# Latents of queries and keys evicted raw, the input norm's factor entered later

## The chip, the cores and the metric

The kernel runs on one core of a Trainium2 chip. The metric is the device time of one execution in microseconds; lower is better. Times in this document are device times of whole runs where they are called so, and otherwise times of the one profiled execution, counted from the start of its span.

## The reference

The whole is a transformer block with a linear recurrence and windowed attention, followed by a second block with latent attention, pooling, cross attention and a mixture of experts, all on 256 tokens of width 1024 in fp32. The change lies at the start of the second block:

```python
hn = rms_norm(h, mix_norm_g[l])            # x * rsqrt(mean(x^2) + EPS) * g
z = hn @ w_in[l]
q_lat, kv_lat, k_rope, u_pool, gate_a, gate_b = jnp.split(z, IN_SPLITS, axis=-1)   # 384, 256, 32, 512, ...
q = (rms_norm(q_lat, q_norm_g[l]) @ w_q_up[l]).reshape(B, S, MLA_HEADS, NOPE_DIM + ROPE_DIM)
q_nope, q_rope = q[..., :NOPE_DIM], q[..., NOPE_DIM:]
q_rope = apply_rope(q_rope, cos[:, :, None, :], sin[:, :, None, :])
kv = (rms_norm(kv_lat, kv_norm_g[l]) @ w_kv_up[l]).reshape(B, S, MLA_HEADS, NOPE_DIM + V_DIM)
k_rope = apply_rope(k_rope, cos, sin)
```

`rms_norm` multiplies each token's row by one factor and each column by a gain. A factor per row commutes with the matrix product, so the kernel multiplies `x * g` by `w_in` and brings in the row's factor after the product.

## The kernel before

Five engines run their own instruction lists, ordered by hand and tied by counting semaphores: SyncE (SP) loads weights, TensorE (PE) multiplies, ScalarE (ACT) and VectorE (DVE) prepare operands and empty the PSUM banks, GpSimd does a few fills. The 256 tokens are two tiles of 128 (`t`).

*Weights.* `plan_units` lists all weight pieces in order. For the stretch at hand they are, in this order, `("lat", 0, 0)`, `("lat", 1, 0)`, `("lat", 0, 1)`, `("lat", 1, 1)`, `("lat", 2, 0)`, `("lat", 2, 1)`, then `w_q_up_2` blocks 0 and 1, `w_kv_up_2` blocks 0 and 1, and eight units `gates2`. In a key the second member is the block of columns and the third the half of the rows: block 0 of `lat` is the 384 columns of the queries' latent, block 1 the 288 of the keys' latent and its rotated part, block 2 the 512 of the pooling branch. A unit lands in one of four raw slots, each split into a high part (`act_hi`, ScalarE, `L936`, into one of three `wh` slots) and a remainder (`dve_lo`, VectorE, `L1459`, into `wl`). `act_unit(key)` and `dve_unit(key)` split the unit that comes **two after** `key`. The split of unit i waits until TensorE has used unit i - 3, and the load of unit i waits for the remainder of unit i - 4.

*Matmuls.* `pe_mm3` issues three matmuls for one product (high by high, high by low, low by high; `L461` to `L463`). `pe_tokens` has tokens as output rows; `pe_features` has features as rows and runs four column groups of four row chunks, 48 matmuls a unit. Its dictionary `at` maps a step (two chunks, six matmuls) to work slipped in ahead of it. Groups alternate between the PSUM banks 4, 5 and 6, 7 (`banks_of`): `("lat", 0)`, `("lat", 2)`, `w_q_up_2` block 1 and `w_kv_up_2` block 1 have 4 and 5; `("lat", 1)`, `w_q_up_2` block 0, `w_kv_up_2` block 0 and `gates2` block 0 have 6 and 7. A group starts when the group two before has been evicted (`freed`).

*Turns.* Activations are transposed by TensorE (`pe_turn`, `L524`) into banks, then split by ScalarE (`act_turn`, `L952`, `turn_hi`) and VectorE (`dve_turn`, `L1514`, `turn_lo`). The turns of the queries' latent (three) and of the keys' (two) share banks 2 and 3, so a third turn waits for the first one's `turn_lo`.

*Norms.* ScalarE sums squares with `accum_out`; VectorE makes the factor by integer shift and three Newton steps (`dve_rsqrt`). `dve_scale("mix2", ...)` makes `rs_of["mix2"]`, the factor of the input norm, after the residual of the first block is complete; its last instruction is `L2120`. `row_mix2` spreads it over a row of a bank for the feature-major eviction of `("lat", 2)` (`RSB`). Before the change, `L1315` and `L1319` evict the two latents to `QL` and `KL` with this factor as `scale`; squares of `QL` and `KL` then give the latents' own factors `rs_of["qk"]`, which enter when `w_q_up_2` (`L1337`) and `w_kv_up_2` (`L1344`, `L1347`) are evicted. The rotated part of the keys is columns 256 to 288 of `KL`, rotated in `dve_rope2_k` (`L1751` to `L1760`) and copied to the eight heads.

Of the kernel before, what the change touches and what calls it, by code (L numbers as in the profile page):

```python
# [14 lines left out]
S = 256  # L15
# [143 lines left out]
def build(nc, A, out):  # L159
    with ExitStack() as ctx:  # L160
# [39 lines left out]
        def v3(t, a, n, off=0):  # L200
            return t[:, off:off + a * n].rearrange("p (a n) -> p a n", a=a)
# [46 lines left out]
        def banks_of(key):  # L248
            return (6, 7) if GN[key] % 2 else (4, 5)

        def evicted(key, n=2):

            before = [k for k in GROUPS[GN[key] % 2:GN[key]:2] if k[0] != "p"]
            return S[f"evict{GN[key] % 2}"], 2 * len(before) + n
# [6 lines left out]
        def scaled(name):  # L261

            return S["rs"], SCALES.index(name) + 1
# [223 lines left out]
        def pe_features(key, r, nu, which, ready=None, at=()):  # L487
            banks = banks_of(key)
            i = U[(*key, r)]
            hi, lo, kc = pe_weights(i)  # L490
            if r == 0:
                PE.wait_ge(*freed(key))
            for c in range(4):
                if i == 0 and c == 2:
                    PE.wait_ge(S["lo"], 1)
                o = PB[banks[c // 2]][:, (c % 2) * 256:(c % 2) * 256 + 256]
                for k in range(kc):
                    if k % 2 == 0 and 2 * c + k // 2 in at:
                        at[2 * c + k // 2]()
                    kk = 4 * r + k  # L500
                    if ready is not None and c == 0:
                        PE.wait_ge(*ready(kk))
                    x, cs_ = slice(kk * 256, kk * 256 + 256), slice(c * 128, c * 128 + 128)
                    m = pe_mm3(o, hi[:, k, cs_], lo[:, k, cs_], TH[which][:, x], TL[which][:, x],
                               r == 0 and k == 0 and c % 2 == 0, r == nu - 1 and k == kc - 1)
            m.then_inc(S["used"], 1)
# [130 lines left out]
        def pe_turn2(q, src):  # L637
            if q == 0:
                PE.wait_ge(S["qrope2"], 2)
                PE.wait_ge(S["row"], 2)  # L640
                PE.wait_ge(S["turn_lo"], TB_["k"] + 2)
            else:
                PE.wait_ge(S["krope2"], 1)
                PE.wait_ge(S["kc"], 4)
            for h in range(8):
                bank = h // 2 % 4
                if h % 2 == 0 and q == 1:
                    PE.wait_ge(S["t2"], bank + 1)
                for t in range(2):
                    m = PE.transpose(PB[bank][0:96, 256 * (h % 2) + 128 * t:256 * (h % 2) + 128 * t + 128], src(t, h), ident)  # L650
                if h % 2:
                    m.then_inc(S["t2_mm"], 1)
# [38 lines left out]
        def pe_main():  # L691
# [137 lines left out]
            def turn_q(c):  # L829
                if c == 0:  # L830
                    PE.wait_ge(*evicted(("lat", 0)))
                    PE.wait_ge(S["turn_lo"], TB_["mix2"] + 8)
                pe_turn("q", QL, (c,), banks=(2, 3))
# [3 lines left out]
                    PE.wait_ge(*evicted(("lat", 1)))  # L837
                pe_turn("k", kvn_src, (c,), banks=(2, 3), free=lambda b: [(S["turn_lo"], TB_["q"] + 3)])

            pe_features(("lat", 2), 0, 2, 0, None, {2: row_mix2, 4: lambda: turn_q(0), 5: lambda: turn_q(1), 7: lambda: turn_q(2)})  # L840
            pe_features(("lat", 2), 1, 2, 0, None, {1: lambda: turn_k(0), 2: lambda: turn_k(1)})
            for b in range(2):
                pe_tokens(("w_q_up_2", b), 0, 1, 1, 0, 384, (lambda kk: (S["turn_lo"], TB_["q"] + kk + 1)) if b == 0 else None)
# [94 lines left out]
        def act_unit(*key):  # L938
            act_hi(U[key] + NW - 1)

        def act_done(key, r):

            ACTE.wait_ge(S["used"], U[(*key, r)] + 1)
# [11 lines left out]
        def act_square(name, n, junk, src):  # L955
            if SQ[name] + n:
                ACTE.wait_ge(S["square"], SQ[name] + n)
            ACTE.activation(junk, src, ACT.Square, accum_out=ssq[name][:, n:n + 1]).then_inc(S["square"], 1)
# [133 lines left out]
        def act_main():  # L1092
# [214 lines left out]
                                    accum_out=ssq["ple"][:, j:j + 1]).then_inc(S["square"], 1)  # L1307
            act_unit("lat", 1, 0)
            act_unit("lat", 0, 1)
            act_unit("lat", 1, 1)  # L1310
            act_unit("lat", 2, 0)
            act_done(("lat", 0), 1)
            ACTE.wait_ge(*scaled("mix2"))
            for t in range(2):
                ACTE.activation(QL[:, t], PB[banks_of(("lat", 0))[t]][:, 0:384], ACT.Copy,  # L1315
                                scale=rs_of["mix2"][:, t:t + 1]).then_inc(evicted(("lat", 0))[0], 1)
            act_done(("lat", 1), 1)
            for t in range(2):
                ACTE.activation(KL[:, t], PB[banks_of(("lat", 1))[t]][:, 0:288], ACT.Copy,  # L1319
                                scale=rs_of["mix2"][:, t:t + 1]).then_inc(evicted(("lat", 1))[0], 1)  # L1320
            ACTE.wait_ge(S["row_mm"], 2)
            ACTE.activation(RSB, PB[0][:, 0:256], ACT.Copy).then_inc(S["row"], 1)
            act_turn("q", range(3), "q_norm_g_2", 1, banks=(2, 3), free=[(S["used"], U["w_ple_proj", 1, 0] + 1)])
            ACTE.wait_ge(*evicted(("lat", 0)))
            for t in range(2):
                act_square("q", t, S1[:, 0:384], QL[:, t, :])
            act_unit("lat", 2, 1)
            act_turn("k", range(2), "kv_norm_g_2", 1, c0=4, banks=(2, 3))
            ACTE.wait_ge(*evicted(("lat", 1)))
# [117 lines left out]
        def dve_then(ins):  # L1447

            steps[0] += 1
            ins.then_inc(S["step_d"], 1)  # L1450

        def dve_after():
            DVE.wait_ge(S["step_d"], steps[0])
# [7 lines left out]
        def dve_unit(*key):  # L1461
            dve_lo(U[key] + NW - 1)
# [287 lines left out]
        def dve_rope2_k():  # L1750
            k1, k2 = KL[:, :, 256:272], KL[:, :, 272:288]  # L1751
            n = [v3(S0, 2, 16, 1536 + 32 * j) for j in range(4)]
            k_ = v3(S0, 2, 32, 1664)
            for o, x, y in ((n[0], k1, c4), (n[1], k2, s4_), (n[2], k2, c4), (n[3], k1, s4_)):
                dve_then(DVE.tensor_tensor(o, x, y, ALU.mult))
            dve_after()
            dve_then(DVE.tensor_tensor(k_[:, :, 0:16], n[0], n[1], ALU.subtract))
            dve_then(DVE.tensor_tensor(k_[:, :, 16:32], n[2], n[3], ALU.add))
            dve_after()
            DVE.tensor_copy(KC[:, :, :, 64:96], k_.unsqueeze(2).to_broadcast([128, 2, 8, 32])).then_inc(S["krope2"], 1)  # L1760

        def dve_m_scores(h):
            mm = mx4[:, 2 * h:2 * h + 2]
# [123 lines left out]
        def dve_main():  # L1887
# [231 lines left out]
            dve_unit("lat", 0, 1)  # L2119
            dve_scale("mix2", ssq["ple"], D, rs_of["mix2"], lambda: DVE.tensor_scalar(mix_hrs, rs_of["mix2"], 0.5, None, ALU.mult))  # L2120
            dve_unit("lat", 1, 1)
            dve_unit("lat", 2, 0)
            dve_turn("q", range(3), "q_norm_g_2", 1, banks=(2, 3))
            dve_unit("lat", 2, 1)
            dve_turn("k", range(2), "kv_norm_g_2", 1, c0=4, banks=(2, 3))
            DVE.wait_ge(S["row"], 2)
            DVE.wait_ge(S["zt"], 1)
            dve_features(("lat", 2), lambda h: UP[:, 2 * h:2 * h + 2, 16:272])
            DVE.wait_ge(S["square"], SQ["k"] + 2)
            dve_rsqrt(rs_of["qk"], [(ssq["q"], 384), (ssq["k"], 256)], last="rs")  # L2130
            dve_unit("w_q_up_2", 0, 0)
            dve_unit("w_q_up_2", 1, 0)
            dve_unit("w_kv_up_2", 0, 0)
# [572 lines left out]
```

## Time and profile before

| what | value |
|---|---|
| median of three timed runs | 1017.94 us (1017.48 to 1020.18) |
| profiled execution, its own time | 1016.1 us |
| span of the profiled execution | 1014.3 us |
| TensorE busy | 977.6 us, 96% |
| VectorE busy | 542.5 us, 53% |
| ScalarE busy | 477.2 us, 47% |
| mean granted TensorE clock | 0.991 of full |
| stretch of `("lat", 2, 0)` on TensorE | 536.47 to 544.78 |

The span runs from the first to the last instruction; the run's own time holds some microseconds around it. Busy time is the union of an engine's instructions. In timelines, `x2` merges two instructions of a line, and what stands in square brackets is idle time of the engine before it and whose instruction ended it.

### The profile page before, as it was taken

The page shows a single profiled execution, that of the slowest core. Times are in us where ns is not written, and L with a number is a line of the kernel's source. Part 1 is how long each engine was busy: PE and PEld are TensorE (multiplying, and loading weights), DVE is VectorE, ACT ScalarE, POOL GpSimd, SP SyncE. Part 2 cuts the span into 40 slices and gives each one's busy share as a digit, 9 for nine tenths or more (in the row PEclk, how much of TensorE's full clock was granted, in tenths as well). Part 3 has the DMA queues.
Part 4 walks back from the last instruction along what each step waited for, and adds up shares of the span by engine and source line. Part 5 has one row for each costly group of instructions (what it writes and reads, how often), then busy time and mean ns, then how long its engine had stood idle before and what let it go on. Part 6 is the DMA issues. An engine that isn't in the chain of part 4 may idle for free.

```text
span 1014.3 us, 13610 instructions
## 1 busy us (share of the span) xinstructions
PE 977.6 (96%) x5479; PEld 743.0 (73%) x5479; DVE 542.5 (53%) x868; ACT 477.2 (47%) x761; POOL 0.8 (0%) x8
## 2 busy tenths in 40 slices
PE   9999998998999999999998999998899999999995
PEld 8879776876889888998898887888774454454442
DVE  5788795665567555554765874764462112112114
ACT  5488555565445444443764765354343222222222
POOL 0000000000000000000000000000000000000000
PEclk9999999999999999999999999999999999999998
DMA  9745466323455544554354744483288999999991
GB/s 300 255 166 168 165 208 206 114 95 125 166 187 167 207 166 167 196 214 150 121 178 134 244 141 135 142 328 91 91 303 279 397 393 393 395 391 396 392 396 51
DMA packets 107268, 223.53 MB, mean 220 GB/s; under 512 B 10185, under 2 KB 15042, under 8 KB 107202
## 3 DMA queue, kind: packets, MB, share of 16 engines
q1 hardware_dynamic: 104752, 219.10, 61.0%
q10 hardware_dynamic: 2450, 3.51, 1.2%
q8 instruction: 46, 0.75, 0.3%
q14 instruction: 20, 0.16, 0.0%
HBM read 221.54 MB, written 1.05 MB: 219 GB/s over the span
## 4 chain that ended last, share of the span: by engine, by line
PE 82%; DVE 9%; ACT 6%; issue 3%; ACTq 0%; POOL 0%; DVEq 0%; POOLq 0%
PE pb L461 17%; PE pb L463 17%; PE pb L462 17%; PE pb L2310 11%; PE pb L2333 6%; PE pb L2285 3%; PE pb L2348 3%; DVE wl L1459 2%; ACT wh L936 2%; PE pb L524 2%; PE pb L595 1%; PE pb L664 1%; PE pb L695 1%; DVE NR L1484 1%; PE pb L2259 1%
## 5 line engine op out<-in xcount | busy, mean ns | idle before, releaser
L1459 DVE TENSOR_TENSOR wl<-raw,wh 128x2048 fp32r<-128x2048 f32 (+2 forms) x113 | 248.8, 2209 | 115.8 <-ACT wh L936 115.6
L936 ACT ACTIVATE wh<-raw 128x2048 fp32r<-128x2048 f32 (+2 forms) x114 | 208.4, 1836 | 125.9 <-PE pb L463 119.8
L461 PE MATMUL pb<-wh,th 128*128 128x512 f32 (+2 forms) x620 | 247.7, 399 | 0.9 <-DVE wl L1459 0.9
L463 PE MATMUL pb<-wh,tl 128*128 128x512 f32 (+2 forms) x620 | 242.0, 390 | 0.0
L462 PE MATMUL pb<-wl,th 128*128 128x512 f32 (+2 forms) x620 | 241.8, 390 | 0.0
L461 PE MATMUL pb<-th,wh 128*128 128x256 f32 x544 | 156.2, 287 | 3.0 <-ACT RC L1315 2.9
L463 PE MATMUL pb<-th,wl 128*128 128x256 f32 x544 | 154.0, 283 | 0.0
L462 PE MATMUL pb<-tl,wh 128*128 128x256 f32 x544 | 153.7, 283 | 0.0
L461 PEld LDWEIGHTS pb<-wh,th 128*128 128x128 f32 x620 | 117.0, 189 | 28.5 <-issue 3.7
L463 PEld LDWEIGHTS pb<-wh,tl 128*128 128x128 f32 x620 | 116.9, 189 | 25.6
L462 PEld LDWEIGHTS pb<-wl,th 128*128 128x128 f32 x620 | 117.1, 189 | 22.8
L461 PEld LDWEIGHTS pb<-th,wh 128*128 128x128 f32 x544 | 103.1, 189 | 6.7 <-issue 5.7
L462 PEld LDWEIGHTS pb<-tl,wh 128*128 128x128 f32 x544 | 103.1, 190 | 0.4
L463 PEld LDWEIGHTS pb<-th,wl 128*128 128x128 f32 x544 | 103.0, 189 | 0.0
L2460 DVE SCALAR_TENSOR_TENSOR S<-S,pb 128x256 f32<-128x256 f32 x16 | 6.7, 421 | 148.4 <-ACT S L2408 148.4
L2408 ACT ACTIVATE S<-pb 128x256 f32<-128x256 f32 x16 | 6.1, 384 | 98.2 <-PE pb L2310 98.2
L2470 DVE TENSOR_TENSOR YL<-pb,YH 128x512 fp32r<-128x512 f32 x32 | 22.1, 692 | 39.3 <-ACT YH L2419 39.3
L2391 ACT ACTIVATE XG<-pb,SM 128x256 f32<-128x256 f32 x64 | 26.7, 471 | 34.9 <-PE pb L2285 33.3
L1514 DVE SCALAR_TENSOR_TENSOR tl<-pb,PC,th 128x256 fp32r<-128x256 f32 x61 | 25.9, 477 | 28.9 <-ACT th L952 28.9
L952 ACT ACTIVATE th<-pb,PC 128x256 fp32r<-128x256 f32 x61 | 24.7, 478 | 34.1 <-PE pb L524 34.1
L2419 ACT ACTIVATE YH<-pb 128x512 fp32r<-128x512 f32 x32 | 19.1, 598 | 43.4 <-PE pb L2333 43.4
L2310 PE MATMUL pb<-raw,XG 128*64 128x512 f32 x160 | 36.1, 595 | 0.0
(359 smaller groups left out, 1091.7 us busy)
## 6 DMA issues: line engine op xcount, KB each, us to landing
raw<-in_w_in SPq DMA_DIRECT2D x31, 1024.0 KB, 5.1
raw<-in_w_up SPq DMA_DIRECT2D x16, 1024.0 KB, 5.6
raw<-in_w_down SPq DMA_DIRECT2D x16, 1024.0 KB, 4.9
raw<-in_w_exp_gate SPq DMA_DIRECT2D x20, 512.0 KB, 10.0
raw<-in_w_exp_up SPq DMA_DIRECT2D x20, 512.0 KB, 11.2
raw<-in_w_exp_down SPq DMA_DIRECT2D x10, 1024.0 KB, 13.8
raw<-in_w_xkv SPq DMA_DIRECT2D x8, 1024.0 KB, 5.0
mwh<-in_w_exp_gate SPq DMA_DIRECT2D x14, 512.0 KB, 11.3
```

The costliest lines, as they stand in the source:

```text
L461: PE.matmul(o, lh, rh, start=start, stop=False, skip_group_check=True)
L462: PE.matmul(o, lh, rl, start=False, stop=False, skip_group_check=True)
L463: return PE.matmul(o, ll, rh, start=False, stop=stop, skip_group_check=True)
L936: ACTE.activation(hi_of(i), raw_of(i), ACT.Copy).then_inc(S["hi"], 1)
L952: ACTE.activation(chunk(TH[which], c0 + c), PB[b][:, 0:256], ACT.Copy, scale=col(gain, c) if gain else scale).then_inc(S["turn_hi"], 1)
L1459: DVE.tensor_tensor(lo_of(i), raw_of(i), hi_of(i).bitcast(F), ALU.subtract).then_inc(S["lo"], 1)
L1514: DVE.scalar_tensor_tensor(chunk(TL[which], c0 + c), PB[banks[c % len(banks)]][:, 0:256], col(gain, c) if gain else scale, chunk(TH[which] ...
L2285: m = PE.matmul(b[:, 256 * k:256 * k + 256], l, s[:, t], start=(k == 0 and t == 0 and i == 0), stop=(t == 1 and i == 1), skip_group_check= ...
L2310: m = PE.matmul(b[64 * j:64 * j + 64, :].rearrange("p (g n) -> p g n", g=2), XG[q % 2][:, c + 64 * j:c + 64 * j + 64], w[:, :, j, k], star ...
L2333: m = PE.matmul(PB[6 + h][64 * j:64 * j + 64, :], HT[p % 2][:, 128 * k + 64 * j:128 * k + 64 * j + 64], w[:, j, 512 * h:512 * h + 512], st ...
L2348: m = PE.matmul(PB[2 * t + h][:, :], SET[p % 4][:, 128 * t:128 * t + 128], YY[p % 2][i][:, 512 * h:512 * h + 512], start=(p == 0 and i == ...
L2391: ACTE.activation(chunk(XG[q % 2], 2 * r + k), gather_bank(q, r)[:, 256 * k:256 * k + 256], ACT.Copy, scale=gffn[:, 2 * r + k:2 * r + k + ...
```

## The change

The evictions of the queries' and keys' latents lose their `scale` and their wait for the input norm's factor, and ScalarE issues that of the queries one split earlier. On TensorE the turns of the queries' latent come at steps 1, 2 and 4 of `("lat", 2, 0)` where they came at 4, 5 and 7, and the row of the factor at step 5 where it came at 2. ScalarE's split of `w_q_up_2` block 0 (`act_unit("lat", 2, 0)`) and the copy to `RSB` move behind the turns and squares of the queries; VectorE's remainder of that unit moves behind the queries' turns. The factor enters in the latents' norm: with s the factor and u the raw latent, s u rsqrt(s^2 mean(u^2) + EPS). The rotated part of the keys is multiplied by s as it is copied to the heads.

```diff
@@ pe_turn2 @@
-                PE.wait_ge(S["krope2"], 1)
+                PE.wait_ge(S["krope2"], 2)
@@ pe_main @@
-            pe_features(("lat", 2), 0, 2, 0, None, {2: row_mix2, 4: lambda: turn_q(0), 5: lambda: turn_q(1), 7: lambda: turn_q(2)})
+            pe_features(("lat", 2), 0, 2, 0, None, {1: lambda: turn_q(0), 2: lambda: turn_q(1), 4: lambda: turn_q(2), 5: row_mix2})
@@ act_main @@
             act_unit("lat", 1, 0)
             act_unit("lat", 0, 1)
+            act_done(("lat", 0), 1)
+            for t in range(2):
+                ACTE.activation(QL[:, t], PB[banks_of(("lat", 0))[t]][:, 0:384], ACT.Copy).then_inc(evicted(("lat", 0))[0], 1)
             act_unit("lat", 1, 1)
-            act_unit("lat", 2, 0)
-            act_done(("lat", 0), 1)
-            ACTE.wait_ge(*scaled("mix2"))
-            for t in range(2):
-                ACTE.activation(QL[:, t], PB[banks_of(("lat", 0))[t]][:, 0:384], ACT.Copy,
-                                scale=rs_of["mix2"][:, t:t + 1]).then_inc(evicted(("lat", 0))[0], 1)
             act_done(("lat", 1), 1)
             for t in range(2):
-                ACTE.activation(KL[:, t], PB[banks_of(("lat", 1))[t]][:, 0:288], ACT.Copy,
-                                scale=rs_of["mix2"][:, t:t + 1]).then_inc(evicted(("lat", 1))[0], 1)
-            ACTE.wait_ge(S["row_mm"], 2)
-            ACTE.activation(RSB, PB[0][:, 0:256], ACT.Copy).then_inc(S["row"], 1)
+                ACTE.activation(KL[:, t], PB[banks_of(("lat", 1))[t]][:, 0:288], ACT.Copy).then_inc(evicted(("lat", 1))[0], 1)
             act_turn("q", range(3), "q_norm_g_2", 1, banks=(2, 3), free=[(S["used"], U["w_ple_proj", 1, 0] + 1)])
             ACTE.wait_ge(*evicted(("lat", 0)))
             for t in range(2):
                 act_square("q", t, S1[:, 0:384], QL[:, t, :])
+            act_unit("lat", 2, 0)
+            ACTE.wait_ge(S["row_mm"], 2)
+            ACTE.activation(RSB, PB[0][:, 0:256], ACT.Copy).then_inc(S["row"], 1)
             act_unit("lat", 2, 1)
@@ dve_rope2_k @@
-            DVE.tensor_copy(KC[:, :, :, 64:96], k_.unsqueeze(2).to_broadcast([128, 2, 8, 32])).then_inc(S["krope2"], 1)
+            for t in range(2):
+                DVE.tensor_scalar(KC[:, t, :, 64:96], k_[:, t].unsqueeze(1).to_broadcast([128, 8, 32]), rs_of["mix2"][:, t:t + 1], None,
+                                  ALU.mult).then_inc(S["krope2"], 1)
@@ dve_main @@
             dve_unit("lat", 1, 1)
+            dve_turn("q", range(3), "q_norm_g_2", 1, banks=(2, 3))
             dve_unit("lat", 2, 0)
-            dve_turn("q", range(3), "q_norm_g_2", 1, banks=(2, 3))
             dve_unit("lat", 2, 1)
...
             DVE.wait_ge(S["square"], SQ["k"] + 2)
-            dve_rsqrt(rs_of["qk"], [(ssq["q"], 384), (ssq["k"], 256)], last="rs")
+            DVE.wait_ge(*scaled("mix2"))
+            rs2 = s2_of["mix2"]
+            dve_then(DVE.tensor_tensor(rs2, rs_of["mix2"], rs_of["mix2"], ALU.mult))
+            dve_after()
+            for name in ("q", "k"):
+                dve_then(DVE.tensor_tensor(ssq[name], ssq[name], rs2, ALU.mult))
+            dve_after()
+            dve_rsqrt(rs_of["qk"], [(ssq["q"], 384), (ssq["k"], 256)])
+            dve_after()
+            DVE.tensor_tensor(v3(rs_of["qk"], 2, 2), v3(rs_of["qk"], 2, 2), rs_of["mix2"].unsqueeze(1).to_broadcast([128, 2, 2]),
+                              ALU.mult).then_inc(S["rs"], 1)
```

## Rows read from the trace of the kernel before

**Rows 1.** The page: engines, costliest groups, DMA issues with time to landing.

```profile
PE 977.6 (96%) x5479; PEld 743.0 (73%) x5479; DVE 542.5 (53%) x868; ACT 477.2 (47%) x761; POOL 0.8 (0%) x8
...
L1514 DVE SCALAR_TENSOR_TENSOR tl<-pb,PC,th 128x256 fp32r<-128x256 f32 x61 | 25.9, 477 | 28.9 <-ACT th L952 28.9
...
raw<-in_w_in SPq DMA_DIRECT2D x31, 1024.0 KB, 5.1
```

**Rows 2.** Waits of TensorE, whole span: total us, times, longest.

```profile
PE pb L461 <- ACT RC L1315: 2.9, 1, 2.9
PE pb L664 <- ACT RC L971: 2.8, 1, 2.8
...
PE pb L524 <- DVE tl L1514: 1.9, 1, 1.9
```

**Rows 3.** Timeline of TensorE, 533 to 545: start, duration, line, operands.

```profile
533.29 0.29 PE L463 MATMUL pb<-wh,tl 128*128 128x288 f32 x1
536.47 0.55 PE L461 MATMUL pb<-th,wh 128*128 128x256 f32 x1 [2.88 <-ACT RC L1315]
...
539.17 0.84 PE L530 MATMUL pb<-CT,SM 128*128 128x128 f32 x4
539.76 0.37 PE L461 MATMUL pb<-th,wh 128*128 128x256 f32 x1
...
541.28 0.38 PE L524 MATMUL pb<-CT,RC 128*128 128x128 f32 x2
...
544.78 0.28 PE L461 MATMUL pb<-th,wh 128*128 128x256 f32 x1
544.90 0.28 PE L462 MATMUL pb<-tl,wh 128*128 128x256 f32 x1
```

**Rows 4.** Timeline of ScalarE, 526 to 537.

```profile
526.88 2.96 ACT L936 ACTIVATE wh<-raw 128x1152 fp32r<-128x1152 f32 x2
530.48 1.92 ACT L936 ACTIVATE wh<-raw 128x2048 fp32r<-128x2048 f32 x1 [0.64 <-PE pb L463]
533.68 1.16 ACT L936 ACTIVATE wh<-raw 128x1152 fp32r<-128x1152 f32 x1 [1.28 <-PE pb L463]
535.27 1.05 ACT L1315 ACTIVATE RC<-pb,SM 128x384 f32<-128x384 f32 x2 [0.43 <-DVE SM L2120]
536.21 0.90 ACT L1319 ACTIVATE KT<-pb,SM 128x288 f32<-128x288 f32 x2
```

**Rows 5.** Timeline of VectorE, 529 to 539.

```profile
529.88 2.29 DVE L1459 TENSOR_TENSOR wl<-raw,wh 128x2048 fp32r<-128x2048 f32 x1 [0.45 <-ACT wh L936]
...
535.00 0.17 DVE L2120 TENSOR_SCALAR SM<-SM 128x2 f32<-128x2 f32 x1
535.08 3.55 DVE L1459 TENSOR_TENSOR wl<-raw,wh 128x2048 fp32r<-128x2048 f32 x2
```

**Rows 6.** Three windows: busy us of each engine, granted clock, DMA share, GB/s.

```profile
182.00:184.00 2.00, 1.49 (x9) 1.27 (x10) 1.33 (x3) 0.88 (x3) 0.00 (x0) 1.00 0.46 109
...
537.00:538.00 1.00, 1.00 (x7) 1.00 (x6) 1.00 (x2) 0.11 (x1) 0.00 (x0) 0.50 0.00 0
...
704.00:706.00 2.00, 1.98 (x5) 1.62 (x6) 0.00 (x0) 0.46 (x1) 0.00 (x0) 0.50 0.12 42
```

**Rows 7.** Timelines of ScalarE, VectorE and TensorE, 554 to 574.

```profile
554.92 1.05 ACT L1337 ACTIVATE RC<-pb,SM 128x384 f32<-128x384 f32 x2 [2.69 <-DVE SM L1490]
...
557.45 1.05 ACT L1337 ACTIVATE RC<-pb,SM 128x384 f32<-128x384 f32 x2 [0.52 <-PE pb L463]
...
560.33 2.29 DVE L1459 TENSOR_TENSOR wl<-raw,wh 128x2048 fp32r<-128x2048 f32 x1 [2.15 <-ACT wh L936]
...
562.83 0.39 PE L461 MATMUL pb<-wh,th 128*128 128x512 f32 x1
...
567.74 0.43 DVE L1760 COPY S<-S 128x512 f32<-128x512 f32 x1
...
573.63 1.91 PE L650 MATMUL pb<-CT,S 128*96 128x128 f32 x16
```

## The prediction

> **What bounds the kernel now.** I read the page first: TensorE is busy for 96% of the span and VectorE and ScalarE for about half each, so time is won only where TensorE stands still or runs slowly [rows 1]. So the second view is the list of TensorE's own waits, where the reader should look for one that the change can touch. The longest of all is: the first matmul of `("lat", 2)` stood 2.9 us behind `L1315`, the eviction of the queries' latents [rows 2]. The third view is TensorE's timeline there. The last matmul of `("lat", 1)` starts at 533.29 (0.13 us apart at this width, so the next could start at 533.42); the first of `("lat", 2)` starts at 536.47. This is 3.05 us from start to start. The twelve matmuls after it, to 539.17, take 2.70 us, 0.21 each; later ones of the same shape start 0.12 apart (twelve are 1.42 us) [rows 3].
>
> Why was `L1315` late? ScalarE's timeline shows a split at 533.68 that ends at 534.84, then a wait of 0.43 for `L2120`, then `L1315` at 535.27 [rows 4]. VectorE's timeline shows `L2120`, the last step of the norm's factor, at 535.00 to 535.17, at the end of a chain that began when the `lo` started at 529.88 was done [rows 5]. `("lat", 0)` itself was finished at about 530.4, when ScalarE was released to its split of 530.48 (the split needs the slot of `("lat", 0, 1)`). `("lat", 0)` and `("lat", 2)` share banks 4 and 5. So the bank was held for 5 us by a factor that the raw copy doesn't need.
>
> The windows give the last piece: the granted clock was 0.50, that is 1.2 of 2.4 GHz, in 537 to 538, right after the idle stretch. It was 0.50 too after the idle of 2.8 us (704 to 706), and stayed 1.00 after one of 1.9 us (182 to 184) [rows 2, 6].
>
> **The change, part by part.**
>
> *Raw evictions, moved ahead of a split.* ScalarE's split of `("lat", 2, 0)` ends at 529.84 (526.88 + 2.96), `("lat", 0)` is done at 530.4, so the two copies of `QL` run from 530.48 to 531.53 at the 1.05 us that they take now. The banks are free 1.9 us before TensorE can use them at 533.42, and the `lo` of its weights is done at 532.17 (529.88 + 2.29) [rows 4, 5]. So the idle time goes: **+3.05**. The split of `("lat", 2, 1)` moves from 530.48 to about 531.4 to 533.4; VectorE takes it up only at 535.08, after the factor, as now, so this costs nothing. If that cover were gone it would be 1 us later, for a matmul group that starts at 541. The copies of `KL` run from 533.68 (where ScalarE is released now by the end of `("lat", 1)`) for 0.9 us; their banks are wanted next by `w_q_up_2`, 13 us later.
>
> *The clock.* Without the idle stretch I expect 1.00 throughout: twelve matmuls in 1.42 and not 2.70 us, **+1.28**. The four small matmuls of `row_mix2` took 0.59 (539.17 to 539.76), partly at the low clock; at best they take half, at worst the same; I take **+0.1** [rows 3].
>
> *The turns of the queries, moved ahead in `("lat", 2, 0)`.* They stood after 24, 30 and 42 matmuls and now stand after 6, 12 and 24, the row after 30. From 541.28 to 544.78 there are three turns and 24 matmuls in 3.50 us, so a turn adds 0.22. TensorE reaches the third turn at 533.42 + 24 x 0.118 + 2 x 0.22 = 536.70. It uses bank 2 again and waits for the `lo` of the first. That one's `hi` is early: the transposes are done at 534.5, ScalarE's `th` follows `KL` at 534.6 and is there at 535.1. But the `lo` is VectorE's, behind the factor (to 535.17) and the `lo` of `("lat", 2, 1)`. That one starts at 535.08 and holds the queue for 2.2 us; the pair of 3.55 us in the rows is it and the 1152-wide one of `w_q_up_2` [rows 5]. So the first turn's `lo` runs from 537.28 for 0.48 us (the mean of 61 such [rows 1]) and TensorE resumes at about 537.88. **A new wait of 1.18, so -1.18.** Queued behind it are the rest of `("lat", 2, 0)` and the row matmuls; ScalarE's `RSB` copy and VectorE's pool features wait for those with microseconds to spare. Bounds for this term: 0 if VectorE came first, 3.05 + 1.28 if something eats all that was won. The value is that of the rows, since each duration in it is shown.
>
> `("lat", 2, 0)` then ends at about 541.5 in place of 544.78.
>
> *The split of `w_q_up_2` block 0, moved from 533.68 to after the third turn and two squares.* It takes 1.16 us [rows 4]. The third `th` is done at 538.7, two squares as wide as the evictions are 1.2 us (0.6 each with their accumulator reads), the split ends at about 541.0, its `lo` at 542.4. TensorE wants it when `("lat", 2)` ends, near 547.5: 5 us of cover. It also frees a raw slot later: the load of the first `gates2` unit is issued near 542.4 and lands 5.1 us after issue at the median [rows 1]; its split is wanted near 555. No cost. Without the cover every microsecond of lateness would be one of TensorE's.
>
> *The factor in the latents' norm.* VectorE gets four small operations (the square of the factor, two products with the sums, the last product with the factor) and the new wait on `mix2`, long met. Dependent small ones come every 0.2 us (0.17 and the gap [rows 5]); two of them are side by side: 0.7 us. So the factor of `L1337` is 0.7 us later, relative to TensorE. That eviction started at 554.92 and was followed by the split that ends before 557.45, where the second one waited 0.5 us for TensorE. The delay therefore eats this 0.5 and leaves 0.1 or so. The place that is tight is the `lo` of the first `gates2` unit: 560.33 + 2.29 = 562.62, against a first matmul at 562.83 [rows 7]. The slack of 0.2 covers the 0.1. I charge **-0.06**; the bounds are 0 and 0.5.
>
> *The rotated part of the keys.* One copy of 0.43 us becomes two multiplications of half its size, at least 0.43 together and at most twice that, so up to 0.4 on VectorE; TensorE asks for the result at 573.63, 5.5 us after the copy's end at 568.17 [rows 7]. Nothing.
>
> Dropping `scale` in four evictions: no row shows a copy of this shape without it. At least nothing, at most 0.1 each, and all are off TensorE's path.
>
> **Sum:** 3.05 + 1.28 + 0.1 - 1.18 - 0.06 = 3.2 us. The next of TensorE's waits that is above 0.3 us is the one of 2.8 before 704 [rows 2], which `w_xq_2`'s eviction ends and which moves with it. Every later load is released by a `lo`, a turn or a used slot, none by an absolute time, so the rest shifts as a block. The profiled execution took 1016.1 us around a span of 1014.3; it would take 1012.9 around 1011.1. It was 1.8 us below the median of the three timed runs (1017.94); taking 3.2 off that gives 1014.7.
>
> **Rivals.**
>
> *A, the forecast*: 1014.7.
>
> *B, the low clock isn't won back.* Either the new wait of 1.2 us pulls the clock down, or the runs without profile often had no low stretch after the old idle time. For it: one profile is one execution, and the clock fell after the two idles of 2.8 and 2.9 us at different delays. Against it: it stayed up after 1.9 us [rows 2, 6]. Then 3.2 - 1.4 = 1.8 us: 1016.1. The Trainium skill ("TensorE: Matmul & The Clock Gate", Part 1, "What's actually happening") says that the monitor runs free of the kernel, so that the number of slow matmuls differs between runs of one kernel. By that rule the 1.4 us would be won in some runs only; no second profile of this kernel is here to show it.
>
> *C, a later low stretch goes too.* With everything moved, the one after 704 might not come. It cost 2 to 3 us at half speed, so up to 1.4 more: 4.6 us in all, 1013.3. The idle of 2.8 us before it stays, which speaks against.
>
> *D, nothing comes of it.* The bank's freeing was not the true last condition and TensorE starts `("lat", 2)` as late as now: 1017.9. Against it: the `lo` is there 4 us before 536.47 [rows 3, 5].
>
> *E, slower.* The load of the first `gates2` unit, issued near 542.4, comes late. It has 12.7 us until its split is wanted. If landing took 14 us, 1.3 would be lost. Slower than now by 0.3% needs a wait of 6.3 us, so a landing of 19 us: 1021. The median landing of 5.1 us speaks against [rows 1].
>
> **How the numbers follow.** A 0.52, B 0.24, C 0.12, D 0.07, E 0.05. About 0.3%, or 3.05 us, is what a measurement of this kernel can tell from no change, and A lies just beyond: with half a microsecond of scatter in each median I give 0.34 of its 0.52 to faster and 0.18 to same. Faster: 0.34 + 0.12 (C) + 0.03 of B = 0.49. Same: 0.18 + 0.21 + 0.07 = 0.46. Slower: 0.05. The range goes from C's 1013.3, less 0.3 of scatter, to beyond B's 1016.1, 1017.0; D and E lie outside with 0.12. A alone is 1013.9 to 1015.5.
>
> **What would show it.** In the profile after: no TensorE wait for the eviction of `QL` before `("lat", 2)`, whose first matmul follows the last of `("lat", 1)` within 0.2 us; clock 1.00 in the 8 us after; one new wait of 1.0 to 1.4 us of a `L524` transpose for `L1514`, near 536.7; `("lat", 2, 0)` 3.3 us earlier; the second `gates2` stretch unshifted against TensorE's own. The prediction would be wrong if the new wait is longer than 1.5 us, if the clock drops behind it, or if a `wl` wait shows up at the start of `gates2`.

## The result and the profile after

| | before | changed | ratio (95% interval) |
|---|---|---|---|
| median of seven runs each | 1017.63 us (1015.61 to 1020.18) | 1011.45 us (1011.09 to 1015.85) | 0.9953 (0.9933 to 0.9973) |
| profiled execution, own time | 1016.1 us | 1011.42 us | |
| its span | 1014.3 us | 1009.6 us | |

The change made the kernel faster by 6.2 us in these medians and by 4.7 us in the profiled executions; the forecast was 3.2, and 1011.45 lies below its range. Line numbers of the changed kernel: `L1312` and `L1316` evict the latents, `L1456` makes the remainders, `L1511` the low parts of the turns, `L1334` evicts `w_q_up_2`, `L2119` is the last step of the factor.

The page after, engines:

```profile
PE 974.7 (97%) x5479; PEld 740.4 (73%) x5479; DVE 543.2 (54%) x873; ACT 476.7 (47%) x761; POOL 0.8 (0%) x8
```

TensorE's waits after, the longest in total (total us, times, longest one):

```profile
PE pb L524 <- DVE tl L1511: 2.9, 2, 1.9
PE pb L664 <- ACT RC L971: 2.8, 1, 2.8
```

The wait of 2.9 for the latent's eviction [rows 2] is gone; the group of turns waiting for VectorE has grown from 1.9 once to 2.9 in two waits. TensorE's timeline after shows the second:

```profile
533.42 0.29 PE L463 MATMUL pb<-wh,tl 128*128 128x288 f32 x1
533.55 0.28 PE L461 MATMUL pb<-th,wh 128*128 128x256 f32 x1
...
534.26 0.38 PE L524 MATMUL pb<-CT,RC 128*128 128x128 f32 x2
...
535.19 0.38 PE L524 MATMUL pb<-CT,RC 128*128 128x128 f32 x2
...
536.72 0.28 PE L463 MATMUL pb<-th,wl 128*128 128x256 f32 x1
537.97 0.44 PE L524 MATMUL pb<-CT,RC 128*128 128x128 f32 x2 [0.96 <-DVE tl L1511]
...
538.95 0.60 PE L530 MATMUL pb<-CT,SM 128*128 128x128 f32 x4
...
541.53 0.28 PE L461 MATMUL pb<-th,wh 128*128 128x256 f32 x1
...
553.99 0.39 PE L461 MATMUL pb<-wh,th 128*128 128x512 f32 x1
...
559.57 0.39 PE L461 MATMUL pb<-wh,th 128*128 128x512 f32 x1
```

The third block follows the second without a gap, and its second half starts at 541.53 where it started at 544.78 [rows 3]; `gates2` starts at 559.57 where it started at 562.83 [rows 7]. ScalarE's and VectorE's timelines after give the reasons:

```profile
530.55 0.88 ACT L1312 ACTIVATE RC<-pb 128x384 f32<-128x384 f32 x2 [0.57 <-PE pb L463]
531.31 1.92 ACT L936 ACTIVATE wh<-raw 128x2048 fp32r<-128x2048 f32 x1
533.75 0.71 ACT L1316 ACTIVATE KT<-pb 128x288 f32<-128x288 f32 x2 [0.53 <-PE pb L463]
```

```profile
535.23 2.28 DVE L1456 TENSOR_TENSOR wl<-raw,wh 128x2048 fp32r<-128x2048 f32 x1
537.43 0.87 DVE L1511 SCALAR_TENSOR_TENSOR tl<-pb,PC,th 128x256 fp32r<-128x256 f32 x2
...
552.07 0.17 DVE L2138 TENSOR_TENSOR SM<-SM 128x4 f32<-128x4 f32 x1
552.15 1.22 DVE L1456 TENSOR_TENSOR wl<-raw,wh 128x1024 fp32r<-128x1024 f32 x1
...
557.11 2.29 DVE L1456 TENSOR_TENSOR wl<-raw,wh 128x2048 fp32r<-128x2048 f32 x1 [1.52 <-ACT wh L936]
...
564.52 0.61 DVE L1758 TENSOR_SCALAR S<-S,SM 128x256 f32<-128x256 f32 x2
```

The first turn's low part starts at 537.43, behind the remainder of `("lat", 2, 1)`, and ends its wait near 537.9. The remainder for `w_kv_up_2` block 0 is done at 553.37 (552.15 + 1.22), 0.62 before TensorE comes to it at 553.99. The remainder for `gates2` is done at 559.40 (557.11 + 2.29), 0.17 before TensorE comes to it, where it was 0.21 [rows 7]. The windows after (busy us of the engines, granted clock, DMA share, GB/s) are 1.00 where the third block runs, and also in 701 to 704, behind the idle time of 2.75 us that ends at 700.79:

```profile
537.00:540.00 3.00, 2.04 (x18) 2.04 (x19) 1.78 (x4) 1.53 (x6) 0.00 (x0) 1.00 0.38 120
701.00:704.00 3.00, 3.00 (x15) 2.64 (x15) 0.86 (x2) 0.48 (x2) 0.00 (x0) 1.00 0.04 14
```

Where did 4.7 us come from? Certain TensorE instructions that end a wait stand in both traces, and distances between them don't depend on the start. From the wait that ends near 248 to the one near 604 it is 355.74 before (603.69 less 247.95) and 352.47 after (600.46 less 247.99): 3.3 us, the forecast's sum. From there to the wait near 1000, 397.01 before (1000.70) and 395.59 after (996.05): 1.4 us, the fall of the clock near 704 [rows 6] that this execution didn't have. (A fall is a stretch with a granted clock of 0.50 inside the kernel.) The table below is built of these two distances, called S1 and S2.

| kernel | S1 | S2 | median, runs | ratio to before (interval) |
|---|---|---|---|---|
| before, first profile | 355.74 | 397.01 | 1017.63, 7 | |
| `before_again` | 355.87 | 397.04 | 1017.82, 11 | 0.9996 (0.9987 to 1.0005) |
| changed, first profile | 352.47 | 395.59 | 1011.45, 7 | 0.9953 (0.9933 to 0.9973) |
| `after_again` | 352.39 | 397.03 | 1014.15, 5 | 0.9963 (0.9950 to 0.9977) |
| `after_third` | 352.35 | 395.60 | 1013.62, 5 | 0.9960 (0.9946 to 0.9974) |
| `raw_only` | 355.10 | 397.34 | 1017.35, 11 | 0.9992 (0.9983 to 1.0001) |
| `factor_later` | 354.31 | 397.29 | 1016.10, 10 | 0.9982 (0.9972 to 0.9991) |
| `late_turns` | 351.87 | 397.38 | 1014.09, 5 | 0.9960 (0.9947 to 0.9974) |
| `late_row6` | 351.17 | 397.35 | 1012.71, 5 | 0.9949 (0.9935 to 0.9962) |
| `warm_536` | 356.44 | 397.23 | 1017.10, 11 | 0.9990 (0.9981 to 1.0000) |
| `warm_536b` | 354.35 | 397.21 | 1015.38, 7 | 0.9974 (0.9963 to 0.9985) |
| `before_warm4` | 354.35 | 395.65 | 1013.41, 5 | 0.9960 (0.9946 to 0.9973) |
| `after_warm701` | 352.44 | 395.58 | 1012.28, 5 | 0.9947 (0.9933 to 0.9960) |
| `after_warm3` | 352.49 | 395.52 | 1011.59, 5 | 0.9938 (0.9924 to 0.9951) |
| `late_row6_warm3` | 351.24 | 395.53 | 1010.43, 5 | 0.9924 (0.9910 to 0.9937) |

S1 repeats within 0.13 us for one kernel, S2 has two values, 397.0 to 397.4 and 395.5 to 395.7. The medians of the changed kernel scatter by more: 1011.45, 1014.15 and 1013.62. Those of the kernel before, in six sets of runs, lie between 1017.63 and 1018.08.

### The profile page after: what moved, and what is told of

Its sections match the earlier page's. It is cut to its first block, busy times and chain, and to the rows that moved or that the text cites. A ratio compares the mean times of both kernels' runs of the same rounds, so it can differ in the third digit from the quotient of the medians.

```text
span 1009.6 us, 13615 instructions
## 1 busy us (share of the span) xinstructions
PE 974.7 (97%) x5479; PEld 740.4 (73%) x5479; DVE 543.2 (54%) x873; ACT 476.7 (47%) x761; POOL 0.8 (0%) x8
## 3 DMA queue, kind: packets, MB, share of 16 engines
HBM read 221.54 MB, written 1.05 MB: 220 GB/s over the span
## 4 chain that ended last, share of the span: by engine, by line
PE 81%; DVE 9%; ACT 6%; issue 3%; ACTq 0%; POOL 0%; DVEq 0%; POOLq 0%
PE pb L461 17%; PE pb L463 17%; PE pb L462 17%; PE pb L2319 11%; PE pb L2342 6%; PE pb L2294 3%; PE pb L2357 3%; DVE wl L1456 2%; ACT wh L936 2%; PE pb L524 2%; PE pb L595 1%; PE pb L664 1%; PE pb L695 1%; DVE NR L1481 1%; PE pb L2268 1%
## 5 line engine op out<-in xcount | busy, mean ns | idle before, releaser
L1456 DVE TENSOR_TENSOR wl<-raw,wh 128x2048 fp32r<-128x2048 f32 (+2 forms) x113 | 248.9, 2209 | 115.7 <-ACT wh L936 115.5
L1511 DVE SCALAR_TENSOR_TENSOR tl<-pb,PC,th 128x256 fp32r<-128x256 f32 x61 | 25.8, 477 | 24.2 <-ACT th L952 24.2
```

What stands on the lines that cost most here:

```text
L1456: DVE.tensor_tensor(lo_of(i), raw_of(i), hi_of(i).bitcast(F), ALU.subtract).then_inc(S["lo"], 1)
L1511: DVE.scalar_tensor_tensor(chunk(TL[which], c0 + c), PB[banks[c % len(banks)]][:, 0:256], col(gain, c) if gain else scale, chunk(TH[which] ...
```

## The experiments

**Both kernels again: `before_again`, `after_again`, `after_third`.** No edit.

> The kernel before, once more, to see how its executions scatter and with how much low clock. Theory K (the clock): TensorE's clock falls after its idle times of 2.7 us and more in most executions, and after those of 1.9 us and less in some; each fall costs about 1.4 us. Then the granted clock of an execution and its time go together (about 3 us of time for 0.003 of mean clock), the times stand in steps of 1.4 us, and the median is above the 1016.1 us of the profiled one, at 1017 to 1018. Rival N (other noise): times scatter by 2 to 4 us with the mean clock unchanged.

> The changed kernel once more. Theory K: the schedule gives 3.3 us, and fewer falls of the clock give the rest: median 1011.3 to 1013, with a mean clock of 0.995 in the fast executions and 0.992 in those of 1015; ratio 0.994 to 0.997. Rival N: the gain is a fixed 6 us that the profile doesn't explain, without relation to the clock.

> The changed kernel a third time. If the falls come by chance of the occasion: executions between 1011 and 1016 again, some near 1011.3 (one fall inside the kernel) and most at 1013 to 1015.5 (two to three), median 1013 to 1015, ratio near 0.9965. If the shift of the schedule keeps the fall near 700 away in a lasting manner: most executions near 1011.4, ratio near 0.9940.

The kernel before gave 1014.91 to 1019.14, with mean clocks of 0.990 to 0.994 and a median of 1017.82, as forecast. The changed one gave 1013.45 to 1015.28 and then 1012.37 to 1014.38; no median as low as the first came back. `after_again` had low windows at 112, 173 and 702, each at 0.50:

```profile
112.00:114.00 2.00, 2.00 (x7) 1.71 (x7) 2.00 (x2) 0.00 (x0) 0.00 (x0) 0.50 0.00 0
173.00:175.00 2.00, 2.00 (x7) 1.21 (x6) 0.78 (x2) 1.55 (x6) 0.00 (x0) 0.50 0.81 190
...
702.00:704.00 2.00, 1.86 (x4) 1.51 (x5) 0.00 (x0) 0.57 (x2) 0.00 (x0) 0.50 0.13 50
```

The first profile of the same program had the one at 173 alone. The profile of `after_again` has a span of 1012.4, 2.8 us more: 1.44 of it is S2, 0.84 the distance from the wait near 110 to that near 248 (138.50 against 137.66, where the low window at 112 lies), 0.54 an arrival at 110 later by as much (110.87 against 110.33), less 0.08 of S1. Theory K had forecast a median of 1011.3 to 1013 here and missed it by 1.2 us; its ratio, 0.994 to 0.997, holds. It also needs an addition that it didn't have: the first 110 us, where the first loads land, scatter by up to 1.7 us (110.33 to 112.03 in the fifteen profiles). That the clock and the time go together step by step didn't hold: one execution of 1018.19 had a mean of 0.992, one of 1017.30 had 0.990. Nor did a fall always cost 1.4 us. The distance from the wait near 110 to that near 248 is 137.57 to 137.85 in the seven profiles whose only fall in it is the one at 170 to 176; a further one near 112 makes it 138.50 (`after_again`), a further one near 185 makes it 138.95 (`warm_536`), so 0.6 to 1.4 more.

**The clock behind the idle time: `warm_536`, `warm_536b`.** The kernel before, with matmuls that nobody reads in the idle time:

```diff
+            def pe_fill(bank, n):
+                for _ in range(n):
+                    PE.matmul(PB[bank][:, 0:256], ident, ROW[:, 0:256], start=True, stop=True, skip_group_check=True)
...
+            PE.wait_ge(S["turn_lo"], TB_["mix2"] + 8)
+            pe_fill(0, 12)          # warm_536b: pe_fill(0, 6)
             pe_features(("lat", 2), 0, 2, 0, None, ...)
```

> The kernel before, with 12 matmuls without use (2.6 us at 0.22 each) put in TensorE's idle time of 2.9 us before the third latent block; nothing moved, nothing raw. Theory K: the granted clock stays 1.00 in 536 to 540, and the block ends 1.4 us earlier: 1.4 us less than before where both have the other falls alike. Rival: the fall of the clock there isn't due to the idle time (or the twelve slow matmuls are slow for another reason, such as operands just written): the clock is 0.50 again and nothing is gained.

> The kernel before with six matmuls without use (0.44 us each by the run with twelve, so 2.6 us) in the idle time of 2.9 us before the third latent block. Theory K (idle time brings the clock down): granted clock 1.00 in 536 to 541, that block 1.4 us shorter; stretch from the last wait near 248 to the one near 604 at 354.4 where the kernel before has 355.7 to 355.9; in time 1.0 to 1.6 less than before. Rival: clock 0.50 again, stretch 355.8.

I had sized the first one wrongly: each such matmul is two instructions of 0.22 us, so twelve ran past the end of the wait. TensorE's timeline of `warm_536`:

```profile
534.98 5.34 PE L694 MATMUL pb<-ROW,CT 128*128 128x256 f32 x24
```

That is 5.3 us in a gap of 3.05, and its S1 is 0.6 longer than before. `warm_536b` fits the gap; its timeline and its windows:

```profile
533.69 2.75 PE L694 MATMUL pb<-ROW,CT 128*128 128x256 f32 x12
536.74 0.36 PE L461 MATMUL pb<-th,wh 128*128 128x256 f32 x1 [0.30 <-ACT RC L1321]
```

```profile
535.00:537.00 2.00, 1.70 (x9) 1.23 (x8) 1.93 (x4) 1.57 (x5) 0.00 (x0) 1.00 0.25 94
537.00:540.00 3.00, 3.00 (x28) 3.00 (x27) 1.91 (x2) 0.77 (x2) 0.00 (x0) 1.00 0.36 98
```

Nothing else changed, the third block started as late as ever, the clock stayed at 1.00 and S1 was 354.35: 1.4 to 1.5 us less, as forecast to 0.1. The low clock was caused by TensorE's idleness and cost its own 1.4. The median fell by more than the forecast 1.0 to 1.6: 2.7 us below the kernel before beside it (1018.08), of which S1 explains 1.4; the rest no trace of this case splits.

**All long idle times filled: `before_warm4`, `after_warm3`, `after_warm701`.** The loop of `pe_fill` with 3 matmuls before the wait near 110 (not shown below), 5 near 168, 6 near 536 (kernel before alone, as above), 5 before the third `pe_m_scores`; `after_warm701` has only the last.

```diff
             def turn_mem(*chunks):
                 if chunks[0] == 0:
+                    PE.wait_ge(S["kq_T"], 6)
+                    pe_fill(2, 5)
                     PE.wait_ge(S["mem_scaled"], 2)
...
                 if h < 2:
+                    if h == 0:
+                        pe_fill(3, 5)
                     pe_m_scores(h + 2)
```

> The kernel before with matmuls without use in four idle times: three of them before the wait near 110 (1.9 us), five before that near 168 (2.7), six before 536 (2.9), five before 701 (2.8); no idle time above 2 us is left. Theory K: the falls of the clock near 171, 537 and 704 go, and that near 111 where it came; 4 to 5 us less than before (1013 to 1014), the executions closer together (within 2 us apart from the first 60 us, where loads arrive differently). Rival (other noise): the scatter of 3 to 4 us stays and the gain is under 3.

> The changed kernel with the same fillings at 110, 168 and 701 (there is no idle time at 536). Theory K: what the change is worth without falls of the clock is the schedule alone, 3.3 less the 1.4 of the fall at 537 that the other kernel no longer has: 1.9 us less than the kernel before with four fillings, so 1011 to 1012. Rival: the change is worth 4 to 6 us also here, so its gain has another source than the wait and the fall.

> The changed kernel with five matmuls without use in the idle time of 2.8 us before 701 only. If the fall there is what parts most executions from the fast ones: 1.4 us less than the changed kernel beside it, where that one has the fall, stretch from the wait near 604 to that near 761 (here some 3 us earlier) at 156.0 and not 157.4. Rival: the other falls come instead, and the median is the changed kernel's.

In `before_warm4` no window but those of the tail, from 1003 on, was below 1.00:

```profile
537.00:540.00 3.00, 3.00 (x28) 3.00 (x27) 1.40 (x2) 0.38 (x1) 0.00 (x0) 1.00 0.53 160
703.00:706.00 3.00, 3.00 (x15) 2.60 (x14) 0.86 (x2) 0.59 (x3) 0.00 (x0) 1.00 0.01 3
```

Its median is 4.7 us below the kernel before beside it. Its profile's span is 3.0 us shorter than that of before (1011.3 and 1014.3): 1.4 in S1, 1.4 in S2, but only 0.3 in the distance from the wait near 110 to that near 248 (137.31 and 137.57), where the fall near 171 went. The other 1.7 us of the median no trace splits. That fillings bring executions closer together is not shown: these five lie within 1.9 us, the eleven of the kernel before beside them within 1.4, and the five of `after_warm3` within 2.5, four of them within 0.8. Against it the changed kernel with fillings is 1.8 us faster (1013.41 less 1011.59; 1.86 in S1), as forecast: 3.3 less 1.4. `after_warm701` is 1.3 below `after_third` on the same chip and occasion. `after_third`'s profile itself lacked the fall there, but its median execution was 1.25 above that profile.

**The arithmetic without the order: `raw_only`.** The changed kernel with every order as before:

```diff
-            act_done(("lat", 0), 1)
-            (the two copies of QL)
             act_unit("lat", 1, 1)
+            act_unit("lat", 2, 0)
+            act_done(("lat", 0), 1)
+            (the two copies of QL)
...
-            pe_features(("lat", 2), 0, 2, 0, None, {1: lambda: turn_q(0), 2: lambda: turn_q(1), 4: lambda: turn_q(2), 5: row_mix2})
+            pe_features(("lat", 2), 0, 2, 0, None, {2: row_mix2, 4: lambda: turn_q(0), 5: lambda: turn_q(1), 7: lambda: turn_q(2)})
```

(the copy to `RSB` and VectorE's turns too.)

> The arithmetic of the change alone (raw latents, factor in their norm and in the keys' rotated part), with every order as before: ScalarE evicts the queries' latent after the splits at 530.5 and 533.7, and turns, row and splits stand where they stood. My theory: the wait for the factor was the last 0.4 us only; the split at 533.7 ends at 534.8, the copies at 535.7, so TensorE starts the third block 0.4 to 0.6 us earlier, still after 2.3 us of idle time with the clock at 0.50 behind it in most executions. Stretch from the wait near 248 to that near 604 at 355.2 to 355.4; time within 1 us of before. Rival: the factor was what held the bank, and taking it out gives most of the 3.3 us by itself.

ScalarE's and TensorE's timelines of `raw_only`, and a window:

```profile
535.18 1.16 ACT L936 ACTIVATE wh<-raw 128x1152 fp32r<-128x1152 f32 x1 [1.28 <-PE pb L463]
536.25 0.85 ACT L1314 ACTIVATE RC<-pb 128x384 f32<-128x384 f32 x2
```

```profile
534.79 0.29 PE L463 MATMUL pb<-wh,tl 128*128 128x288 f32 x1
537.25 0.36 PE L461 MATMUL pb<-th,wh 128*128 128x256 f32 x1 [2.16 <-ACT RC L1314]
```

```profile
538.00:542.00 4.00, 4.00 (x23) 4.00 (x22) 2.14 (x2) 0.38 (x1) 0.00 (x0) 0.58 0.47 133
```

The copies now wait for nothing but the split ahead of them, yet TensorE is idle for 2.16 us and the clock falls. S1 gains 0.7, a little more than the 0.4 to 0.6 that I had forecast; the rest of the change's gain needs the eviction ahead of the splits. No run has that order with the factor still in the copy, but the rows bound it: the factor came at 535.17 and the copy started at 535.27 [rows 4, 5], so the order alone could have brought it forward by 0.1 us at most (an estimate).

**Later factor: `factor_later`.** Ten more dependent operations before the last product of the latents' factor:

```diff
+            for _ in range(10):
+                dve_then(DVE.tensor_tensor(rs2, rs_of["mix2"], rs_of["mix2"], ALU.mult))
+                dve_after()
             DVE.tensor_tensor(v3(rs_of["qk"], 2, 2), ...
```

> The changed kernel with ten more small dependent VectorE operations (2.0 us) before the last product of the latents' factor, so 2.7 us more than in the kernel before and not 0.7. My theory: after the first 0.7 us the slack before w_kv_up_2's banks and the gates2 remainder is used up: TensorE waits 1.2 to 2.0 us in all in 553 to 562, at w_kv_up_2 block 0 first. The changed kernel's 0.7 us then was covered with little left. Rival: there is ample slack behind the factor, and no wait appears.

TensorE's timeline of `factor_later`:

```profile
556.78 0.47 PE L461 MATMUL pb<-wh,th 128*128 128x512 f32 x1 [1.27 <-DVE wl L1456]
...
562.75 0.50 PE L461 MATMUL pb<-wh,th 128*128 128x512 f32 x1 [0.16 <-DVE wl L1456]
```

S1 is 1.9 longer than in the changed kernel for 2.0 us of delay. The first wait is for the remainder of `w_kv_up_2` block 0, which VectorE makes after the factor, the second for that of `gates2`. The sizes fit the slacks that the changed kernel has there, 0.62 and 0.17: of 2.0 us of delay all but the smaller of the two is lost. So the 0.7 of the change itself had room, and hardly any more is left, at `gates2` above all.

**The new wait: `late_turns`, `late_row6`, `late_row6_warm3`.**

```diff
-            pe_features(("lat", 2), 0, 2, 0, None, {1: lambda: turn_q(0), 2: lambda: turn_q(1), 4: lambda: turn_q(2), 5: row_mix2})
+            pe_features(("lat", 2), 0, 2, 0, None, {2: row_mix2, 4: lambda: turn_q(0), 5: lambda: turn_q(1), 7: lambda: turn_q(2)})    # late_turns
+            pe_features(("lat", 2), 0, 2, 0, None, {4: lambda: turn_q(0), 5: lambda: turn_q(1), 6: row_mix2, 7: lambda: turn_q(2)})    # late_row6
```

> The changed kernel with TensorE's turns of the queries and the row back at their old steps (row at 2, turns at 4, 5, 7); all else as changed. My theory: the new wait of 1.0 us before the third turn goes, no other comes, since the second turn's and the keys' orders have slack: another 1.0 us, and 1.0 to 1.2 us less than the changed kernel at equal clock. Rival: the turns arrive late at ScalarE, the split of w_q_up_2 block 0 comes behind them, and TensorE waits for its remainder at the end of the latents: no gain, or a loss up to 1 us.

> The changed kernel with turns at 4, 5, 7 and row at 6, without fillings. My theory: no new wait in the third latent block, 1.0 us less than the changed kernel where the falls of the clock are alike; stretch from the wait near 248 to that near 604 at 351.4 (352.4 in the changed kernel); median between 1010.5 and 1013.5, as the falls come. Rival: as the changed kernel.

> The changed kernel with the turns of the queries at their old steps 4, 5 and 7, the row at 6, and the three fillings. The run with the row at 2 showed that it then waits 0.24 us for the factor. My theory: neither wait is left, 1.0 us less than the changed kernel with fillings: 1010 to 1011, the fastest of all. Rival: the end of the latents waits for the remainder of w_q_up_2 block 0, and nothing is gained.

`late_turns` gained 0.5 in S1, half of what I expected: with the turns out of the way the row came before its factor, and waited for it, as its timeline shows:

```profile
538.35 0.71 PE L530 MATMUL pb<-CT,SM 128*128 128x128 f32 x4 [0.24 <-DVE SM L2119]
```

The profile marks 0.24 as idle; the third block as a whole is 0.5 longer than in `late_row6` (13.55 against 13.03 us from the last matmul of `("lat", 1)` to the first of `w_q_up_2`). Its median was that of the changed kernel beside it (1014.09 and 1014.15). With the row at step 6 no wait is left in the block and S1 is 351.17, 1.2 below the changed kernel. With the fillings this is the fastest version measured: 1010.43 us, ratio 0.9924 (0.9910 to 0.9937).

## Why the prediction was wrong, by its own steps

*Raw evictions, +3.05: right.* The copies ran at 530.55, the bank was free before 533.55. They took 0.88 us where 1.05 was charged, off the path.

*The clock, +1.28 and +0.1: right.* `warm_536b` has it alone: 1.4 to 1.5 in S1, where the two terms make 1.38.

*The new wait, -1.18: right in place and cause, a little large.* It ended at 537.97 (537.88 forecast), 1.13 us after the time at which TensorE was ready (536.84, one matmul after 536.72). The profile calls 0.96 of it idle, because the last matmul's end is counted.

*The factor in the norm, -0.06: it cost nothing.* The 0.7 us was there: the chain of small operations runs from 549.16 to 552.24, 3.1 us where it took 2.4 (552.41 to 554.83). No TensorE wait came. The tight place was the one that I named: the `gates2` remainder has 0.17 us of slack left, that of `w_kv_up_2` block 0 has 0.62. By my own rows the slack of 0.2 covered the 0.1, so there was no ground for a charge.

*The keys' rotated part, nothing: right.* 0.61 us where the copy took 0.43 [rows 7], over at 565.1, and TensorE's turn of the keys (its first record here is at 570.4) was not late.

*The sum, 3.2: right to 0.3* as a statement on this stretch (S1 is 3.3 to 3.5 less in three profiles of the changed kernel against two of before). `warm_536b` shows the clock's part alone and `late_row6` (S1 1.2 less without the turns' wait and the row's) the part of the new wait.

*The step that failed is how the sum was carried to the medians.* I wrote that the profiled execution "was 1.8 us below the median of the three timed runs (1017.94); taking 3.2 off that gives 1014.7". This supposes that the median of the changed kernel, too, lies 1.8 us above its profiled execution, and that this execution has the same falls of the clock as the one before, outside the stretch. Neither was so. The profiled execution took 1011.42 where the sum had 1012.9: it is 1.5 us lower, and 1.4 of that is the fall near 704 which it didn't have (S2). And the median of those seven runs is 1011.45, 0.03 above it and not 1.8. The two parts together, 1.5 and 1.8, are the 3.25 us between 1014.7 and 1011.45. The mean clocks go with the second part: four of the seven executions, 1011.09 to 1011.45, had 0.995 like the profiled one, and the other three, 1013.69 to 1015.85, had 0.992 to 0.994. Of 73 executions of the kernel before whose clock is on record, 46 had 0.990 or less, under the 0.991 of its profiled one. So the profiled execution of before spent less time at the low clock than most, and that of the changed kernel was like most of its set. How much of the 1.8 is falls and how much the scatter of the first 110 us stays open: no execution other than the profiled ones has a trace.

Rival C had the mechanism of the first part (the fall near 704 is missing), and 1011.5 follows from it for the profiled execution; but I priced it from the median of before, at 1013.3, gave it 0.12, and let the range end there. I also gave each median half a microsecond of scatter. The six medians of before keep to that (0.45 us in all), the three of the changed kernel don't (2.7 us). The falls differ between executions of one program: the changed kernel's first profile has one low stretch inside, at 173, `after_again` has three, at 112, 173 and 702. Of the unfilled idle times of 2.2 to 2.9 us in the fifteen profiles 23 of 26 had a fall behind them, of those of 1.9 us 5 of 26 (near 112 in two profiles, near 185 in three). I had counted such differences against the gain only, in rival B; they widen the range on both sides. The Trainium skill ("TensorE: Matmul & The Clock Gate", Part 1, "What's actually happening") says that the count of slow matmuls differs between runs of one kernel. The traces agree: three falls in one execution of the changed kernel, one in another.

Part of the miss is the luck of the draw. Over all its 17 executions on three occasions the changed kernel's median is 1013.69 (1011.09 to 1015.85), inside my range; nine of the ten later ones had mean clocks of 0.991 to 0.993. Over 80 of before it is 1017.86. This is 4.2 us, of which S1 has 3.4; the rest would fit fewer falls elsewhere, which is argued and not shown. The shift alone doesn't keep the fall near 700 away: `after_again` is the same program and has it, behind the same idle time of 2.75 us. Whether the shift makes it rarer is open: it was missing in two of three profiles of the changed kernel, and there in all eight of other kernels that left this idle time unfilled, also in those shifted by as much or more.

## What to carry to other kernels

When an eviction holds a bank, ask which of its inputs the copy needs and what stands ahead of it in its engine's queue: here taking the factor out gave 0.7 us of S1, and the new order, with the copy ahead of two splits, the other 2.6 to 2.8. An idle time of TensorE can cost more than itself: of those of 2.2 to 2.9 us here, 23 of 26 had a stretch of low clock behind them, and near 537 and 704 this took another 1.4 us. If such an idle time can't be scheduled away, matmuls without use can fill it: at these two places they won the 1.4 back, and between 110 and 248 two fillings together were worth 0.3 to 0.6. Compare two kernels by the distance between events that both have, and carry a sum to a median only with the scatter that single executions show, and with the clocks of all of them beside that of the profiled one.

## What was not expected of the hardware

ScalarE's copy out of a bank is shorter without a factor per partition: two of 128x384 took 0.88 us where they took 1.05, two of 128x288 took 0.71 where they took 0.90 [rows 4]. The product with a factor per partition on VectorE, with a repeated source, took 0.61 us for 512 elements in two instructions where the plain copy took 0.43 in one [rows 7]. A low stretch was not always as long: in `raw_only` one lasted from 170.0 to about 176.8, twice as long as any other between 10 and 1000 us in the fifteen profiles:

```profile
170.00:176.00 6.00, 5.25 (x16) 4.06 (x17) 2.67 (x4) 4.12 (x12) 0.00 (x0) 0.50 0.50 175
176.00:177.00 1.00, 1.00 (x5) 0.90 (x4) 0.00 (x0) 0.40 (x1) 0.00 (x0) 0.58 0.00 0
```
